# A decoder layer with convolution, differential attention and routed experts: the third modulation set moves from TensorE to GpSimd, the attended values come half a head later, and the q and k norm weights are folded

## What is computed

```python
mod = silu(c) @ w_ada + b_ada                    # 6 x 1024: shift1, scale1, gate1, shift2, scale2, gate2
h = rms_norm(x, norm1_g) * (1 + scale1) + shift1
u_conv, q, k, v, g = split(h @ w_in)
y_conv = silu(layer_norm(causal_depthwise_conv31(a * sigmoid(gt)))) @ w_conv_out + b
q = partial_rope(rms_norm(q, q_norm_g)); k = partial_rope(rms_norm(k, k_norm_g))   # 16 of 64 channels rotate
o = (softmax(q1 k1) - lam * softmax(q2 k2)) @ v    # 8 heads, causal
y_attn = (rms_norm(o, subln_g) * 0.8) @ w_attn_out
x = x + gate1 * ((sigmoid(g_conv) * y_conv + sigmoid(g_attn) * y_attn) @ w_o)
h = rms_norm(x, norm2_g) * (1 + scale2) + shift2
x = x + gate2 * moe(h)                           # top 4 of 32 experts, clamped SwiGLU
```

## Time and profile before

| what | value |
|---|---|
| median of 3 runs | 1286.09 us (1285.32 to 1287.28) |
| the profiled execution | 1285.43 us, span 1283.7 us |
| TensorE busy | 1081.6 us (84% of the span) |
| VectorE busy | 403.8 us (31%) |
| ScalarE busy | 219.0 us (17%) |
| GpSimd busy | 52.6 us (4%) |
| read from HBM | 473.03 MB, 369 GB/s over the span |

### The profile page before, as it was taken

How to read it: one execution, slowest core, us unless ns; L and a number is a source line. 1 busy time by engine, 2 the same in 40 slices (tenths; PEclk the granted TensorE clock), 3 DMA queues, 4 the chain that set the end, 5 groups by cost and what they waited for, 6 DMA issues and landing times.

```text
span 1283.7 us, 23436 instructions
## 1 busy us (share of the span) xinstructions
PE 1081.6 (84%) x9958; PEld 528.9 (41%) x9958; DVE 403.8 (31%) x1129; ACT 219.0 (17%) x461; POOL 52.6 (4%) x95
## 2 busy tenths in 40 slices
PE   8999999899998566569998667978669696999976
PEld 5864458788433121224443222423224142444432
DVE  1388997621232111112222111212112121232221
ACT  1111124640121000012111000201012110121110
POOL 2000000355000000000000000000000000000000
PEclk9999999999999888889999878989989898999997
DMA  9998672256889999999999999999999999699997
GB/s 329 345 371 331 238 286 93 105 181 230 321 334 428 428 426 428 427 427 428 426 429 425 429 426 430 414 428 428 425 429 426 428 426 429 249 429 427 427 427 311
DMA packets 66084, 475.81 MB, mean 371 GB/s; under 512 B 6329, under 2 KB 19966, under 8 KB 39390
## 3 DMA queue, kind: packets, MB, share of 16 engines
q1 hardware_dynamic: 62100, 471.36, 89.4%
q0 software_dynamic: 816, 1.84, 0.5%
q10 hardware_dynamic: 3098, 1.56, 0.5%
HBM read 473.03 MB, written 1.05 MB: 369 GB/s over the span
## 4 chain that ended last, share of the span: by engine, by line
PE 49%; DMA 40%; SPq 5%; ACT 3%; DVE 1%; another core or an unknown queue 1%; issue 1%; ACTq 0%; DVEq 0%
DMA weights<-in_w_down 23%; DMA weights<-in_w_up 16%; PE bank L1566 13%; PE bank L1594 7%; PE bank L1297 7%; PE bank L1290 6%; SPq L466 4%; PE bank L1282 2%; PE bank L1435 2%; PE bank L1507 2%; PE bank L1233 2%; PE bank L1494 1%; PE bank L1203 1%; DMA weights<-in_w_ada 1%; PE bank L1514 1%
## 5 line engine op out<-in xcount | busy, mean ns | idle before, releaser
L1566 PE MATMUL bank<-weights,buf_d 128*32 128x512 f32 x3008 | 392.7, 668 | 140.4 <-DMA weights<-in_w_up 140.4
L1566 PEld LDWEIGHTS bank<-weights,buf_d 128*32 128x32 f32 x3008 | 96.3, 117 | 403.0 <-DMA weights<-in_w_up 210.6
L1594 PE MATMUL bank<-weights,buf_d 128*32 128x256 f32 x3008 | 179.5, 385 | 43.0 <-DMA weights<-in_w_down 40.0
L1174 DVE TENSOR_SCALAR u_conv<-bank 128x256 f32<-128x256 f32 x47 | 20.0, 425 | 464.5 <-PE bank L1566 464.5
L782 ACT ACTIVATE u_conv<-u_conv 128x256 f32<-128x256 f32 x47 | 19.6, 417 | 709.1 <-DVE u_conv L1174 709.1
L1594 PEld LDWEIGHTS bank<-weights,buf_d 128*32 128x32 f32 x3008 | 91.3, 111 | 117.1 <-DMA weights<-in_w_down 52.0
L872 DVE SCALAR_TENSOR_TENSOR weights<-u_conv,weights 128x256 f32<-128x256 f32 x240 | 97.8, 480 | 0.5
L1290 PE MATMUL bank<-weights,buf_d 128*128 128x512 f32 x192 | 82.9, 594 | 0.0
L1186 DVE TENSOR_TENSOR buf_d<-bank,u_conv 128x256 f32<-128x256 f32 x47 | 20.0, 425 | 182.3 <-PE bank L1594 182.3
L782 ACT ACT_TABLE_LOAD x47 | 60.3, 1283 | 1.4 <-issue 0.5
L1297 PE MATMUL bank<-buf_d,weights 128*128 128x256 f32 x256 | 58.6, 383 | 0.0
(11 more groups left out here) (275 smaller groups left out, 800.6 us busy)
## 6 DMA issues: line engine op xcount, KB each, us to landing
weights<-in_w_up SPq DMA_DIRECT2D x128, 2048.0 KB, 35.5
weights<-in_w_down SPq DMA_DIRECT2D x64, 2048.0 KB, 39.3
weights<-in_w_in SPq DMA_DIRECT2D x10, 2048.0 KB, 15.7
weights<-in_w_ada SPq DMA_DIRECT2D x8, 2048.0 KB, 19.3
weights<-in_w_ada SPq DMA_DIRECT2D x8, 1024.0 KB, 11.3
weights<-in_w_in SPq DMA_DIRECT2D x8, 512.0 KB, 10.2
weights<-in_w_in SPq DMA_DIRECT2D x4, 1024.0 KB, 13.0
weights<-in_w_conv_out SPq DMA_DIRECT2D x2, 2048.0 KB, 11.6
```

The source lines that it names most:

```text
L1566: ins = t.matmul(UP[SLOTS * g:SLOTS * g + SLOTS, :], xgT[:, r, SLOTS * j:SLOTS * j + SLOTS], up_group(w[:, r, :], g), start=False, stop=(j ...
L1594: ins = t.matmul(DOWN[rows, 0:T], actT[:, r, at:at + SLOTS], w[:, g, r, T * q:T * q + T], start=False, stop=(h == 1 and g == 1 and r == 1))
```

## The change

- **Third modulation set.** The 32 matmuls between k and v are gone. GpSimd multiplies each of the eight 128 x 2048 slices of the set by its column of `silu(c)` and adds it to the running sum, in place in the ring: eight TENSOR_SCALAR and seven TENSOR_TENSOR. After the v tiles TensorE sums the last slice over its partitions with four matmuls against ones. A block is given back to SP when GpSimd's sums have passed it (`mod_summed`). The bias row (`ada_row(1)`) comes 50 conv instructions later on VectorE, and the second transpose of the modulation (`turn_rows(1)`) stands behind the q and k transposes on TensorE.
- **Norm weights.** For the channels that don't rotate, the product of both norm weights scales k at the copy out of its transposes (ScalarE). For the rotating ones the weights are multiplied into the rotation tables once (six VectorE instructions), and the rotation has four instructions instead of six. The multiplication L939 is gone. Four small loads are added on ScalarE's queue at the start.
- **Attended values.** `attend(h - 2)` stands behind the scores of head h, where `attend(h - 1)` stood behind its gates. The copy out no longer waits for ScalarE's squares, and these are taken from SBUF after the heads, behind the first half of the gates' sigmoid. The first tile of `conv_out` stands between the last two `attend`s.

```diff
-        rot = early[:, 3584:3840].rearrange("p (i g j) -> p i g j", i=4, g=8)
+        rot = early[:, 3584:3840].rearrange("p (i g j) -> p i g j", i=2, g=8)
+        turns = early[:, 3968:4096].rearrange("p (w i t h j) -> p w i t h j", w=2, i=2, t=TT, h=2)
...
-        order += [("ada", 1)] + [("v", i) for i in range(4)] + [("mod2T", 0), ("mod2T", 1)] + [("qkT", i) for i in range(8)]
-        for h in range(HEADS + 1):
-            if h < HEADS:
-                order += [("gate", h)]
+        order += [("v", i) for i in range(4)] + [("ada", 1), ("mod2T", 0)] + [("qkT", i) for i in range(8)] + [("mod2T", 1)]
+        for h in range(HEADS):
+            if h >= 2:
+                order += [("o", h - 2)]
+            order += [("gate", h)]
             if h:
-                order += [("aT", h - 1), ("o", h - 1)]
+                order += [("aT", h - 1)]
             if h == MEAN_AT:
                 order += [("mean", 0)]
             if h == VAR_AT:
                 order += [("var", 0)]
-        order += [("y_conv", i) for i in range(3)] + [("oT", i) for i in range(4)] + [("y_conv", 3)]
+        order += [("o", HEADS - 2), ("aT", HEADS - 1), ("y_conv", 0), ("o", HEADS - 1)]
...
-            for gi in range(2):
-                used[ADA0[gi] + i] = (ada_done, 3 * gi + i + 1)
+            used[ADA0[0] + i] = (ada_done, i + 1)
+            used[ADA0[1] + i] = (mod_summed, 2 * i + 3)
...
+            pool.wait_ge(c_ready, 1)
+            for k in range(KD):
+                w, seen = (blk(ADA0[1] + j // 2, 2)[:, j % 2, :] for j in (k, max(k - 1, 0)))
+                if k % 2 == 0:
+                    pool.wait_ge(blk_full[place(ADA0[1] + k // 2)], 16 * loads_before[ADA0[1] + k // 2])
+                ins = g.tensor_scalar(w, w, c_act[:, k, 0:1], None, ALU.mult)
+                if k == 0:
+                    ins.then_inc(mod_summed, 1)
+                else:
+                    ins.then_inc(mod_scaled, 1)
+                    pool.wait_ge(mod_scaled, k)
+                    pool.wait_ge(mod_summed, k)
+                    g.tensor_tensor(w, w, seen, ALU.add).then_inc(mod_summed, 1)
...
+            for i, w in enumerate((q_norm_g, k_norm_g)):
+                for half in range(2):
+                    load(col_rows[26 + i:27 + i, HD * half:HD * half + HD], w, in_cols)
...
-                s.copy(dst, bank(QKT_USE + i)[:, :].rearrange("p (h t) -> p h t", h=2)).then_inc(
-                    bank_free[(QKT_USE + i) % 4], 1)
+                src = bank(QKT_USE + i)[:, :].rearrange("p (h t) -> p h t", h=2)
+                ins = s.copy(dst, src) if i < 4 else s.activation(dst, src, ACT.Copy, scale=cols[:, 28:29])
+                ins.then_inc(bank_free[(QKT_USE + i) % 4], 1)
...
+                freed(act_e, o_use(h))
                 for tt in range(TT):
-                    s.activation(qk_junk[:, P * tt:P * tt + P], bank(use)[:, P * tt:P * tt + P], ACT.Square,
+                    if h:
+                        act_e.wait_ge(o_ready, 2 * h + tt - 1)
+                    s.activation(qk_junk[:, P * tt:P * tt + P], o_tok[:, tt, VD * h:VD * h + VD], ACT.Square,
...
-                    attended(h - 1)
...
-            attended(HEADS - 1)
+
+            def open_gates(i):
+                s.activation(gates[:, KD * i:KD * i + KD, :], gates[:, KD * i:KD * i + KD, :], ACT.Sigmoid).then_inc(gate_ready, 1)
+
+            open_gates(0)
+            for h in range(HEADS):
+                attended(h)
             act_e.wait_ge(o_ready, 2 * HEADS)
             s.activation(rstd[:], ssq[:], ACT.Sqrt, scale=1.0 / VD, bias=eps[:]).then_inc(o_ready, 1)
-            for i in range(2):
-                s.activation(gates[:, KD * i:KD * i + KD, :], gates[:, KD * i:KD * i + KD, :], ACT.Sigmoid).then_inc(gate_ready, 1)
+            open_gates(1)
...
+                    step(v.tensor_tensor(cols[:, 28:29], cols[:, 26:27], cols[:, 27:28], ALU.mult))
+                    for half in range(2):
+                        step(v.memset(cols[HD * half:HD * half + ROT, 28:29], 1.0))
...
+            for which in range(2):
+                gain_rot = qk_g[:, which, 0:ROT].rearrange("p (h j) -> p h j", h=2)
+                places = [P, TT, 2, HALF]
+                step(v.tensor_tensor(turns[:, which, 0, :, :, :], rope[:, 6, :, :].unsqueeze(2).to_broadcast(places),
+                                     gain_rot.unsqueeze(1).to_broadcast(places), ALU.mult))
+                step(v.tensor_tensor(turns[:, which, 1, :, :, :], rope[:, 7, :, :].unsqueeze(2).to_broadcast(places),
+                                     gain_rot.unsqueeze(1).to_broadcast(places), ALU.mult))
+                step(v.tensor_scalar(turns[:, which, 1, :, 1, :], turns[:, which, 1, :, 1, :], -1.0, None, ALU.mult))
...
-                step(v.tensor_tensor(dst, dst, qk_g[:, which, :].unsqueeze(1).to_broadcast([P, 8, HD]), ALU.mult))
-                cos = rope[:, 6, tt, :].unsqueeze(1).to_broadcast([P, 8, HALF])
-                sin = rope[:, 7, tt, :].unsqueeze(1).to_broadcast([P, 8, HALF])
-                x1, x2 = dst[:, :, 0:HALF], dst[:, :, HALF:ROT]
-                v.tensor_tensor(rot[:, 0, :, :], x1, cos, ALU.mult)
-                v.tensor_tensor(rot[:, 1, :, :], x2, sin, ALU.mult)
-                v.tensor_tensor(rot[:, 2, :, :], x2, cos, ALU.mult)
-                step(v.tensor_tensor(rot[:, 3, :, :], x1, sin, ALU.mult))
-                v.tensor_tensor(x1, rot[:, 0, :, :], rot[:, 1, :, :], ALU.subtract)
-                v.tensor_tensor(x2, rot[:, 2, :, :], rot[:, 3, :, :], ALU.add).then_inc(qk_ready, 1)
+                x = dst[:, :, 0:ROT]
+                for j in range(2):
+                    turn = turns[:, which, j, tt, :, :].rearrange("p h j -> p (h j)").unsqueeze(1).to_broadcast([P, 8, ROT])
+                    ins = v.tensor_tensor(rot[:, j, :, :], x, turn, ALU.mult)
+                step(ins)
+                for j in range(2):
+                    ins = v.tensor_tensor(dst[:, :, HALF * j:HALF * j + HALF], rot[:, 0, :, HALF * j:HALF * j + HALF],
+                                          rot[:, 1, :, HALF - HALF * j:ROT - HALF * j], ALU.add)
+                ins.then_inc(qk_ready, 1)
                 for stretch in between[i]:
                     conv(*stretch)
-            ada_row(1)
             conv(2, 17, TAPS)
             conv(3, 0, 11)
+            ada_row(1)
...
-                if h:
-                    keep_o(h - 1)
+                if h >= 2:
+                    keep_o(h - 2)
...
-            keep_o(HEADS - 1)
...
+            keep_o(HEADS - 2)
...
+            dve.wait_ge(gate_ready, 1)
+            mix_conv(0)
+            keep_o(HEADS - 1)
+            mix_conv(1)
+            dve.wait_ge(o_ready, 2 * HEADS + 1)
+            freed(dve, o_use(HEADS - 1))
+            step(v.reciprocal(rstd[:], rstd[:]))
+            v.tensor_tensor(o_tok[:].rearrange("p t (h e) -> p (t h) e", h=HEADS),
+                            o_tok[:].rearrange("p t (h e) -> p (t h) e", h=HEADS),
+                            rstd[:].unsqueeze(2).to_broadcast([P, 16, VD]), ALU.mult).then_inc(on_ready, 1)
+            for i in (2, 3):
+                mix_conv(i)
...
-            fill(pe, ADA_USE[1])
-            for i in range(4):
-                ada_rows(ADA_USE[1], ADA0[1], i)
...
+            fill(pe, ADA_USE[1])
+            pe.wait_ge(mod_summed, KD)
+            total = blk(ADA0[1] + 3, 2)[:, 1, :]
+            for gi in range(4):
+                ins = t.matmul(bank(ADA_USE[1])[32 * gi:32 * gi + 32, :], ones[:, 0:32], total[:, NB * gi:NB * gi + NB],
+                               start=True, stop=True)
+            ins.then_inc(bank_full[ADA_USE[1] % 4], 1)
+            turn_rows(0)
...
+            turn_rows(1)
...
+                if h >= 2:
+                    attend(h - 2)
...
+            attend(HEADS - 2)
+            turn(HEADS - 1)
             pe.wait_ge(swish_ready, KD)
-            for i in range(3):
+            conv_out(0)
+            attend(HEADS - 1)
+            for i in (1, 2):
```

More of the change, by code:

```diff
@@ L267, in build @@
                              "oh_ready", "units_ready"))
-        mod_ready, ebias_ready, conv_sum, tables_kept = (
-            sem(n) for n in ("mod_ready", "ebias_ready", "conv_sum", "tables_kept"))
+        mod_ready, ebias_ready, conv_sum, tables_kept, mod_scaled, mod_summed = (
+            sem(n) for n in ("mod_ready", "ebias_ready", "conv_sum", "tables_kept", "mod_scaled", "mod_summed"))
         pick_ready, pickw_ready, sel_ready, gathered, xs_ready, xt_done, xm_ready, cmb_ready = (
@@ L358, in build @@
                 order += [("var", 0)]
-        order += [("y_conv", i) for i in range(3)] + [("oT", i) for i in range(4)] + [("y_conv", 3)]
+        order += [("o", HEADS - 2), ("aT", HEADS - 1), ("y_conv", 0), ("o", HEADS - 1)]
+        order += [("y_conv", i) for i in (1, 2)] + [("oT", i) for i in range(4)] + [("y_conv", 3)]
         order += [(name, i) for name in ("y_attn", "w_o") for i in range(4)]
@@ L961, in _ @@
```

(11 more changed lines are left out.)

12 lines of the change are left out of this document (1 added, 11 removed).

## The result

| | before | after |
|---|---|---|
| median, lowest and highest | 1286.34 us (1285.32 to 1287.28) | 1331.08 us (1329.79 to 1332.12) |
| ratio, with its 95% interval | | 1.0348 (1.0335 to 1.036) |
| span of the profiled execution | 1283.7 us | 1328.3 us |
| VectorE busy | 403.8 us | 450.0 us |
| GpSimd busy | 52.6 us | 129.3 us |

What follows compares the result with a forecast made beforehand. VectorE and TensorE were taken to reach head 0 together, with the front's shift carried to the end. Terms -5.5 + 45 - 2.5 - 4.3 = +32.7 on 1285.4 gave 1318 us, range 1300 to 1333.

Steps and rivals of the forecast that it cites:

- What bounds, and the carry: Expert loads wait for TensorE's progress behind the heads, so a shift of the front reaches the end one for one.
- VectorE, relieved: VectorE before head 0: norm multiplication -5.8, shorter rotation -1.2, six added table operations +1.5, sum -5.5 us.
- GpSimd's own time: Eight scalings of 2.7 us and seven additions of 4.1 on GpSimd: 50.3 us, with ends 45.7 and 65.5.
- What VectorE loses: VectorE's two-SBUF-input instructions wait at the shared ports for GpSimd's whole instructions: 45 us lost, bounds nothing and 60.
- the overlap: Part of GpSimd's 50.3 us that VectorE can still use: 3 us without second SBUF input, 2 at instruction starts.
- Head 0: VectorE reaches head 0's maxima at 226, 39.5 us later; the scores stand at 222, before it asks.
- Run-ahead and heads: TensorE does gates while VectorE is behind, -2.5 us; `attend` no longer waits for copied probabilities in the heads, -4.3.
- Ports cost nothing: Rival: the ports cost VectorE next to nothing, head 0 comes 5.5 us earlier, 1275 to 1276 us, faster; chance 0.13.
- VectorE keeps the ports: Rival: VectorE's queue is served first, GpSimd finishes late and TensorE waits for `mod_summed`: 1313 us, slower; chance 0.15.
- What would show it: Signs: GpSimd between 105 and 165 us, conv instructions of 2 to 4 us, TensorE idle over 15 us, expert part shifted.

Runs made afterwards that it cites:

- pe_third: The changed kernel with the third modulation set, its bias row and transposes back on TensorE in their old places: 1283.70 us, 0.9983 of before.
- norm_alone: The kernel before with only the norm weights folded: 1286.44 us, 1.0005 of before.
- two_op: The changed kernel with GpSimd's scaling written as a multiplication and an addition of a tiny constant: 1316.93 us, 1.0247 of before.
- attended_alone: The kernel before with only the attended values half a head later: 1283.77 us, 0.9984 of before.
- memsets: The changed kernel with GpSimd's 15 scalings and additions replaced by 31 memsets that only write, third set not computed: 1281.94 us, 0.997 of before.
- thin_one_op: The changed kernel with each conv tap but the first on 8 of 256 columns in four of eight tiles: 1303.55 us, 1.0137 of before.

## Why the prediction was right in direction and 12 us short

**What bounds, and the carry.** Right. The heads end 44.1 us later and the span 44.6, one for one.

**VectorE, relieved: -5.5.** Between before and `pe_third`, VectorE leaves the last q/k tile at 155.53 and at 148.75: -6.8, near enough. `norm_alone` shows that by itself it is worth nothing.

**GpSimd's own time: 50.3.** This is the term that was mis-sized: 77.0 was measured, beyond my upper end of 65.5. Of the 26.7 us too little, 23.5 are the scaling ("I take 2.7, between this and the casts"; 5.6 measured) and 3.2 the addition (4.1; 4.56 measured). For the addition the Trainium skill (GPSIMD Engine Reference, Performance versus the Vector engine) has 4497 ns, and the trace is close to it. I took the row of 0.572 us for 256 columns for the same form because it has the same name, TENSOR_SCALAR. It isn't: L567 of the kernel before multiplies and adds, two operations, and the new scaling has one. For two operations my 2.7 was fair, as `two_op` shows with 2.42. No row of the kernel before has the one-operation form, so its price could not be read from the trace, and not even the upper end, 4.6, covered it.

**What VectorE loses: 45.** 51.7 measured, 6.7 more. The mechanism stands. The loss grew much less than GpSimd's time because the overlap, guessed at 5 us, was 25: GpSimd lets go some 1.9 us before the end of each of eight scalings (15 us), and the rest is mostly work without a second SBUF input. Four tiles came by while GpSimd was busy (their scaling out of PSUM, L972, is at 116.03, 132.06, 152.31 and 181.48), not one or two, and at my 2 us each they make 8 of these 10. That the range held is luck: my own sum with 77.0 in place of 50.3 gives 1345, outside it, and only the overlap that I had too small brought the time back to 1331.

**Head 0: -39.5 later at 226.** 232.94: the +44.9 of VectorE, and 1.4 more, 1.0 of it because the scores came after it had asked for them. I had them ready at 222, counting some 2 us from the end of the bias row to the scores; the transposes of k wait for its bank, then 3.7 us of transposes, ScalarE and scores follow until 232.9, 7.9 in all. In this path stand also the scaled copies of k, which I had put at the price of the plain ones: on ScalarE (L704) four with a scale took 687 ns each and four plain ones 587.

**Run-ahead and heads: -2.5 and -4.3.** Only 2.2 came, from maxima to the transposes behind the heads (46.35 to 44.1); `attended_alone` gives 2.0 to 2.6 by itself. The wait of 4.3 went, as forecast, but two of 1.1 and 0.7 came, both for VectorE's copy of the attended values; the 2.5 left fit the 2.2. TensorE did its gates while it waited, yet head 0's first transpose came 47 us later than before, not less: nothing of the 2.5 arrived.

Together: 6.7 - 1.3 for VectorE, 1.4 for the scores, 4.6 for the heads and 0.5 behind them make 11.9 of the 12.0 us between forecast and measurement.

**The rivals.** *Ports cost nothing*: refuted by conv's 11.88 us for 4.17, and `memsets` (1281.9) is what that case would have looked like, with 1275 too hopeful. *VectorE keeps the ports*: refuted; GpSimd's rows follow one another without a gap, and VectorE gets in one instruction beside each addition and, beside each one-operation scaling, one and then four or five more in its last 1.9 us. TensorE waited for VectorE's banks, not for `mod_summed`, except in `thin_one_op`.

**What would show it.** GpSimd's end was to be 165 and was 186; the single conv instructions of 3.9 to 4.7 us were to be 2 to 4; four tiles came by for one or two; TensorE's idle time, the shift of the expert part, and the waits' names came as said.

## What to carry to other kernels

Moving elementwise work that reads SBUF to an idle GpSimd is not free while VectorE has instructions with two SBUF inputs: each of GpSimd's instructions is then a wait for the one that stands beside it, as long as GpSimd holds the ports and whatever the waiting instruction's own size. Less work on VectorE helps only through the slack that it leaves. Price an operation from a row of its own form, which is the operations inside the instruction and not only its name; where there is no such row, say so in the range, and try the other form: here one more operation in the scaling made GpSimd 26 us and the kernel 14 us faster. Take a change of several parts apart even when it loses as a whole; with the set back on TensorE it is 1283.7 against 1285.6 for the kernel before in the same runs.

## What the runs showed that I had not expected

- GpSimd scales 2048 columns by a scalar per partition in 5.6 us with one operation and in 2.1 to 2.4 with two, both beside full conv and with conv's instructions down to 8 columns. Why one operation costs more was not tried.
- The one-operation scaling lets VectorE in about 1.9 us before its end, at 2048 and at 1024 columns; the addition and the two-operation scaling hold to within 0.2 us of it. Why was not tried.
- A VectorE instruction of 8 columns waits as long as one of 256, and seven two-input instructions in a row lose hardly more than four (52.5 us against 51.7 in all).
- GpSimd's memsets, 55.6 us of them, leave two-input instructions alone, but two first taps of conv took 3.81 us instead of 0.74 beside them.
